# First attention of a two-block kernel: keys rotated on GpSimd, four tiles turned by VectorE blocks and GpSimd transfers, and one pair of late sums four units apart

## What is computed

```python
mod = (c @ w_mod[l] + b_mod[l]).reshape(B, N_MOD, D)
h = rms_norm(x, g_pre_mix[l]) * (1 + scale_m) + shift_m
proj = h @ w_in[l]
q_lat = rms_norm(proj[..., COL_QLAT:COL_K], q_lat_norm_g[l])
q = apply_rope((q_lat @ w_q_up[l]).reshape(B, S, ATTN_HEADS, HEAD_DIM), cos_a, sin_a)
k = apply_rope(proj[..., COL_K:COL_V].reshape(B, S, ATTN_HEADS, HEAD_DIM), cos_a, sin_a)
...
y_b = dsa_attention(q, k, v, q_idx, k_idx, idx_w)
gates = jax.nn.sigmoid(proj[..., COL_GATE:])
merged = gates[..., :D] * (y_a @ w_proj_a[l]) + gates[..., D:] * (y_b @ w_proj_b[l])
```

## Time and profile before

| | |
|---|---|
| median of 3 runs | 2350.73 us (2349.63 to 2352.76) |
| the profiled execution, own time | 2351.91 us |
| its span, first to last instruction | 2350.2 us |
| TensorE busy | 2333.5 us (99%) |
| VectorE busy | 1672.9 us (71%) |
| ScalarE busy | 1124.1 us (48%) |
| GpSimd busy | 415.2 us (18%) |
| mean granted TensorE clock | 0.999 of full speed |

### The profile page before, as it was taken

One profiled execution on the slowest core, in us unless ns is written; L12 is line 12 of the kernel. 1 busy time (PEld: TensorE's weight loads), 2 busy tenths in 40 slices (PEclk: granted clock), 3 DMA queues, 4 the chain that ended last, 5 costly groups with the idle time before them and its releaser, 6 DMA issues.

```text
span 2350.2 us, 31106 instructions
## 1 busy us (share of the span) xinstructions
PE 2333.5 (99%) x10647; PEld 1930.8 (82%) x10647; DVE 1672.9 (71%) x2138; ACT 1124.1 (48%) x1415; POOL 415.2 (18%) x824
## 2 busy tenths in 40 slices
PE   9999999999999999999999999999999999999998
PEld 7888788888888888888888888888888888888887
DVE  7998899999886666665544465676765577888764
ACT  4544546543554444444443445544744444544554
POOL 0001000024001211212100001111112135686310
PEclk9999999999999999999999999999999999999999
DMA  9985469999847877865655556666566666665564
GB/s 392 396 318 203 154 241 360 332 343 369 350 171 250 268 251 237 270 232 195 235 193 195 192 179 219 215 218 215 183 209 215 204 209 198 201 197 191 184 212 153
DMA packets 174106, 561.05 MB, mean 239 GB/s; under 512 B 29696, under 2 KB 34080, under 8 KB 173344
## 3 DMA queue, kind: packets, MB, share of 16 engines
q1 hardware_dynamic: 145584, 528.28, 65.1%
q0 software_dynamic: 25600, 22.33, 3.2%
q10 hardware_dynamic: 2800, 8.81, 1.1%
HBM read 534.91 MB, written 2.11 MB: 229 GB/s over the span
## 4 chain that ended last, share of the span: by engine, by line
PE 89%; DVE 6%; DMA 2%; issue 1%; ACT 1%; SPq 0%; ACTq 0%; DVEq 0%
PE acc L2409 27%; PE acc L2410 27%; PE acc L2416 27%; DVE lo L1397 2%; DVE macc L1433 2%; PE tb L2497 1%; DMA raw<-in_wa_dram 1%; DMA start_raw<-in_wa_dram 1%; PE tb L2940 1%; PE tb L2409 1%; PE tb L2410 1%; PE tb L2416 1%; PE acc L2467 0%; PE acc L2465 0%; PE acc L2466 0%
## 5 line engine op out<-in xcount | busy, mean ns | idle before, releaser
L1397 DVE TENSOR_TENSOR lo<-raw,hi 128x1024 fp32r<-128x1024 f32 x809 | 969.3, 1207 | 549.7 <-ACT hi L723 546.3
L723 ACT ACTIVATE hi<-raw 128x1024 fp32r<-128x1024 f32 x809 | 844.7, 1049 | 978.5 <-PE acc L2416 690.7
L2409 PE MATMUL acc<-hi,Hh 128*128 128x512 f32 x1960 | 773.7, 395 | 1.8 <-issue 0.9
L2410 PE MATMUL acc<-hi,Hl 128*128 128x512 f32 x1960 | 763.6, 390 | 0.0
L2416 PE MATMUL acc<-lo,Hh 128*128 128x512 f32 x1960 | 524.4, 389 | 0.0
L2409 PEld LDWEIGHTS acc<-hi,Hh 128*128 128x128 f32 x1960 | 368.1, 188 | 80.0 <-issue 4.8
L2416 PEld LDWEIGHTS acc<-lo,Hh 128*128 128x128 f32 x1960 | 367.9, 188 | 77.3
L2410 PEld LDWEIGHTS acc<-hi,Hl 128*128 128x128 f32 x1960 | 368.2, 188 | 75.9 <-issue 1.4
L2409 PE MATMUL acc<-hi,hbh 128*128 128x512 f32 x512 | 202.7, 396 | 0.0
L2410 PE MATMUL acc<-hi,hbl 128*128 128x512 f32 x512 | 199.6, 390 | 0.0
L638 POOL DMA_DIRECT2D tok<-sgt x176 | 86.2, 498 | 501.1 <-DVE sgt L1523 424.4
(11 more groups left out here) (374 smaller groups left out, 2270.7 us busy)
## 6 DMA issues: line engine op xcount, KB each, us to landing
raw<-in_wa_dram SPq DMA_DIRECT2D x680, 512.0 KB, 4.4
late_raw<-in_wa_dram SPq DMA_DIRECT2D x96, 512.0 KB, 6.0
raw<-in_wb_dram SPq DMA_DIRECT2D x96, 512.0 KB, 4.2
start_raw<-in_wa_dram SPq DMA_DIRECT2D x64, 512.0 KB, 7.7
raw<-in_wc_dram SPq DMA_DIRECT2D x64, 512.0 KB, 4.1
tok<-sgt POOLq DMA_DIRECT2D x384, 32.0 KB, 4.4
landed<-sgt POOLq DMA_DIRECT2D x192, 32.0 KB, 4.0
pt_landed<-att_parts POOLq DMA_DIRECT2D x192, 12.0 KB, 3.0
```

What stands on the lines that cost most here:

```text
L723: act.activation(hi[:, s, 0:n], raw[:, r, 0:n], ACT.Copy).then_inc(hi_ready, 1)
L1397: dve.tensor_tensor(lo[:, s, 0:n], raw[:, r, 0:n], hi[:, s, 0:n].bitcast(F32), ALU.subtract)\
L2409: pe.matmul(dst(tt), a, hi[:, s, w], start=first and i == 0, stop=False)
L2410: pe.matmul(dst(tt), b, hi[:, s, w], start=False, stop=False)
```

## The change

The two key parts are rotated in place by GpSimd (rotate_keys) as soon as they are summed; the first ahead of the index keys, the second behind them. For the two query tiles VectorE does the products and GpSimd the add (add_query). Each of the four tiles is then turned into blocks by VectorE (turn_first), moved by 16 transfers of GpSimd's queue and put in order into kT or qT by two copies on GpSimd (move_first). The buffers lie in sg. TensorE's four tiles of transposes and ScalarE's eight copies out of PSUM go. ScalarE waits for all four tiles before the first sigmoid, TensorE before the scores of head 0. Block 5's second half is transposed one unit later, after OUT0+26, and its two takes move to before OUT0+25 and OUT0+29.

```diff
-LATE_SUMS = [LATE[b * KD + KD - 1] + (6 if 2 <= b < 5 else 3) * half for b in range(LATE_WIDE) for half in range(2)]
-TAKES = [unit + 5 for unit in LATE_SUMS]
+LATE_SUMS = [LATE[b * KD + KD - 1] + (6 if 2 <= b < 5 else 4 if b == 5 else 3) * half for b in range(LATE_WIDE) for half in range(2)]
+TAKES = [unit + (3 if i // 2 == 5 else 5) for i, unit in enumerate(LATE_SUMS)]
...
+QIDX_TURNED = KX_COPIED + 3, KX_COPIED + 5
+KEYS_SUMMED = (QUARTERS - 1) * PARTS // 2 + 2
...
+        first_out = [sb(f"first_out{i}", [P, 4, TT * P], at=sg_at + (8 + 4 * i) * KB) for i in range(2)]
+        first_in = [sb(f"first_in{i}", [P, 4, TT * P], at=sg_at + (16 + 4 * i) * KB) for i in range(2)]
+        key_tmp = [sb(f"key_tmp{i}", [P, TT, N], at=sg_at + (16 + 4 * i) * KB) for i in range(2)]
...
+            def rotate_keys(n):
...
+                for tt in range(TT):
+                    pool.wait_ge(acc_free[tt], KEYS_SUMMED + n)
+                pool.tensor_tensor(tmp[:, :, :, 0:half], a[:, :, :, half:HD], spread(ropeS[:, :, 0:half]), ALU.mult)
+                pool.tensor_tensor(tmp[:, :, :, half:HD], a[:, :, :, 0:half], spread(ropeS[:, :, half:HD]), ALU.mult).then_inc(key_step, 1)
+                pool.wait_ge(key_step, 2 * n + 1)
+                pool.tensor_tensor(a, a, spread(ropeC[:]), ALU.mult).then_inc(key_step, 1)
+                pool.wait_ge(key_step, 2 * n + 2)
+                pool.tensor_tensor(a, a, tmp, ALU.add).then_inc(first_rotated, 1)
+
+            pool.wait_ge(const_in, 5 * 16)
+            rotate_keys(0)
             pool.wait_ge(rstd_ready, 3)
...
             pool.tensor_copy(kd[:, :, IDIM:], kd[:, :, 0:IDIM]).then_inc(kidx_ready, 1)
+            rotate_keys(1)
+
+            def move_first(n):
+
+                pool.wait_ge(first_blocks, n + 1)
+                if n > 1:
+                    pool.wait_ge(first_turned, n - 1)
+                for i in range(4):
+                    for j in range(4):
+                        pool.dma_start(first_in[n % 2][32 * j:32 * j + 32, i, :], first_out[n % 2][32 * i:32 * i + 32, j, :])\
+                            .then_inc(first_moved, 16)
+                pool.wait_ge(first_moved, MOVED * (n + 1))
+                dst, k = (kT, qT)[n // 2], n % 2 * 4
+                for tt in range(TT):
+                    at = slice(tt * P, (tt + 1) * P)
+                    ins = pool.tensor_copy(dst[:, k:k + 4, at].rearrange("p k (i t) -> p k i t", i=4),
+                                           first_in[n % 2][:, :, at].rearrange("p i (k t) -> p k i t", k=4))
+                ins.then_inc(first_turned, 1)
+
+            def add_query(t):
+
+                pool.wait_ge(query_parts, t + 1)
+                pool.tensor_tensor(tok[:, 1 - t], tok[:, 1 - t], sgt[:], ALU.add).then_inc(query_added, 1)
+
+            move_first(0)
+            add_query(0)
+            move_first(1)
+            add_query(1)
+            move_first(2)
+            move_first(3)
...
-            copy_tile(kT, 0)
-            split_to(QI3B + 2)
-            copy_tile(kT, 4)
...
-                if i == 6:
-                    copy_tile(qT, 0)
...
-                if i == 10:
-                    copy_tile(qT, 4)
...
                 if since == 0 and n >= 0:
+                    if n == 0:
+                        act.wait_ge(first_turned, 4)
                     finished(GATES0 + 8 * n + 7)
                     read_out(lambda tt: sg[:, tt, n * N:(n + 1) * N], n % 2, ACT.Sigmoid)
...
-            for tt in range(TT):
-                dve.wait_ge(acc_free[tt], (QUARTERS - 1) * PARTS // 2 + 2)
-            rotate(None, lambda tt: tok[:, 1, tt, :], 4, HD, HD // 2, ropeC, ropeS, src=lambda tt: part_at(0, tt))
...
-            for tt in range(TT):
-                dve.wait_ge(acc_free[tt], (QUARTERS - 1) * PARTS // 2 + 3)
-            rotate(None, lambda tt: tok[:, 0, tt, :], 4, HD, HD // 2, ropeC, ropeS, src=lambda tt: part_at(1, tt))
+
+            def turn_first(n):
+
+                if n < 2:
+                    dve.wait_ge(first_rotated, n + 1)
+                    src = lambda tt: part_at(n, tt)
+                else:
+                    dve.wait_ge(query_added, n - 1)
+                    dve.wait_ge(first_moved, MOVED * (n - 1))
+                    src = lambda tt: tok[:, 3 - n, tt, :]
+                for tt in range(TT):
+                    at = slice(tt * P, (tt + 1) * P)
+                    ins = dve.transpose(first_out[n % 2][:, :, at].rearrange("p j (k t) -> p j k t", k=4),
+                                        src(tt).rearrange("p (k j c) -> p j k c", k=4, j=4))
+                ins.then_inc(first_blocks, 1)
...
-                dve.wait_ge(tr_copy, TOK_TURNED[t])
-                dve.wait_ge(tok_ready, t + 2)
+                if t > 1:
+                    dve.wait_ge(tr_copy, QIDX_TURNED[t - 2])
+                if t == 3:
+                    dve.wait_ge(query_added, 1)
+                elif t > 0:
+                    dve.wait_ge(tok_ready, t)
...
-                    rotate(0, tile, 4, HD, HD // 2, ropeC, ropeS)
+                    rotate(0, tile, 4, HD, HD // 2, ropeC, ropeS, add=False)
+                    for tt in range(TT):
+                        dve.wait_ge(acc_free[tt], KEYS_SUMMED + 2 + t)
+                    dve.sem_inc(query_parts, 1)
...
             add_uv(4)
+            turn_first(0)
             turn_query(1)
+            turn_first(1)
...
+                if i == 9:
+                    turn_first(2)
...
             split_to(GATES0 + 10)
+            turn_first(3)
...
-            part_tile(q3, 0, after={1: lambda: turned(1)})
+            part_tile(q3, 0)
...
-            part_tile(q3, 1, after={0: lambda: turned(0)})
+            part_tile(q3, 1)
...
-            tile(qlath, qlatl, 0, 2, after={0: lambda: query_turned(1, 6), 1: lambda: logits(7)})
+            tile(qlath, qlatl, 0, 2, after={0: lambda: logits(6), 1: lambda: logits(7)})
...
+                if head == 0:
+                    pe.wait_ge(first_turned, 4)
...
-                if u == GATES0:
-                    turned(0)
```

More of the change, by code:

```diff
@@ L149 @@
 KX_COPIED = KD // 2 + 1
-TOK_TURNED = KX_COPIED + 2, KX_COPIED + 4, KX_COPIED + 7, KX_COPIED + 9
-COPIES_BEFORE_K2 = TOK_TURNED[3] + 4 + HEADS1
+QIDX_TURNED = KX_COPIED + 3, KX_COPIED + 5
+COPIES_BEFORE_K2 = QIDX_TURNED[1] + HEADS1
+KEYS_SUMMED = (QUARTERS - 1) * PARTS // 2 + 2
 QB = A_UNITS
@@ L410, in two_blocks @@
         merged_tok = sem("merged_tok")
+        key_step = sem("key_step")
+        first_rotated = sem("first_rotated")
+        query_parts = sem("query_parts")
+        query_added = sem("query_added")
+        first_blocks = sem("first_blocks")
+        first_moved = sem("first_moved")
+        first_turned = sem("first_turned")
         hid_blocks = sem("hid_blocks")
@@ L595, in _ @@
                                pattern=[[0, 8], [1, P]], channel_multiplier=-1).then_inc(ws_ready, 1)
+            def rotate_keys(n):
+                heads = lambda ap: ap.rearrange("p t (h d) -> p t h d", h=4)
+                spread = lambda ap: ap.unsqueeze(2).to_broadcast([P, TT, 4, ap.shape[-1]])
+                half = HD // 2
+                a, tmp = heads(k_part[:, n]), heads(key_tmp[n][:])
+                for tt in range(TT):
[8 more added lines that the diff above has]
+            rotate_keys(0)
             pool.wait_ge(rstd_ready, 3)
@@ L607, in _ @@
             ih = IROPE // 2
-            pool.wait_ge(const_in, 5 * 16)
             pool.wait_ge(kn_step, 3)
@@ L1494, in layer_norm_stats, with rotate @@
                 inverse_root()
-            def rotate(pair, dst, heads, dim, half, cos, sin, width=N, src=None, done=tok_ready):
+            def rotate(pair, dst, heads, dim, half, cos, sin, width=N, src=None, done=tok_ready, add=True):
                 h4 = lambda ap: ap.rearrange("p (h d) -> p h d", h=heads)
@@ L1512, in rotate @@
                         ins.then_inc(acc_free[2 * pair + tt], 1)
+                if not add:
+                    return
                 for tt in range(TT):
```

## The result

| | kernel before | changed kernel |
|---|---|---|
| median of 5 runs | 2350.73 us (2349.58 to 2352.76) | 2360.86 us (2359.75 to 2363.78) |
| ratio, 95% interval | | 1.0042 (1.0031 to 1.0054) |
| the profiled execution, own time | 2351.91 us | 2363.78 us |
| its span | 2350.2 us | 2362.1 us |
| mean granted TensorE clock | 0.999 | 0.997 |

The account below looks back on a forecast made before the run. TensorE was taken to bound the kernel. Transposes -3.5, standstill +7.6, clock +1.7 and late sums -1.0 gave +4.8 us, with VectorE and GpSimd's queue at nothing: 2355.5 us against the median of 2350.73, range 2350.0 to 2359.5.

Parts of the forecast that it names:

- The bound: Whole kernel: TensorE, busy 2333.5 of 2350.2 us, sets the time; any new gap is paid in full.
- Transposes, -3.5 us: Four tiles of transposes removed from TensorE, 0.87 us each, all on the path: 3.48 us won.
- VectorE, nothing: VectorE's changed work costs nothing: net relief in a stretch where TensorE never waited for it.
- Rival 3: VectorE and GpSimd hold each other up, as at 207 to 280 us: 4 us lost, 2359.5 us; chance 0.13.
- GpSimd's queue, hidden: GpSimd's queue before the last tile costs 0: tile 3 finds it free with 4 us to spare.
- The standstill, +7.6 us: TensorE stands still before unit GATES0+11 while ScalarE waits for the last tile: 7.6 us, bounds 2.6 to 9.4.
- The clock, +1.7 us: TensorE's clock falls to 1.2 GHz behind the standstill, costing 1.7 us, bounds 0 and 2.7.
- The late sums, -1.0 us: Block 5's moved sums remove TensorE's 1.46 us wait at 642.78; 0.45 is lost again: 1.0 won, bounds 0.3 and 1.46.
- Sum: All terms together: +4.8 us, 2355.5 us against the median, range 2350.0 to 2359.5.

Follow-up runs that it names:

- cut: Changed kernel with GpSimd's key rotations and query additions cut into pieces of 128 elements a partition (24 and 8 instructions); 2354.43 us, ratio 1.0008.
- rot_dve: Changed kernel with both key rotations and both query additions back on VectorE, GpSimd keeping transfers and copies; 2357.82 us, ratio 1.0025.
- turns_spread: rot_dve with VectorE's block transposes of query tile 2 behind logits step 7 and tile 3 behind step 11; 2351.83 us, ratio 1.0002.
- pool_reads: Kernel before plus four scratch additions of two 128x1024 SBUF tiles on GpSimd behind its index keys; 2357.30 us, ratio 1.0025.
- warm_gap: Changed kernel with 60 unused transposes on TensorE behind unit GATES0+10, where it stood still; 2360.68 us, ratio 1.0040.
- tile3_early: Changed kernel with VectorE's block transposes of tile 3 moved from behind the GATES0+9 split to behind the twelfth logits step; 2355.36 us, ratio 1.0017.
- turns_early: rot_dve with VectorE's block transposes of query tile 2 behind logits step 5 and tile 3 behind step 9; 2351.90 us, ratio 1.0001.
- cut_spread: cut with VectorE's block transposes of tile 2 behind logits step 7 and tile 3 behind step 11; 2349.88 us, ratio 0.9991.
- after_again: The changed kernel itself run and traced once more; 2361.16 us, ratio 1.0039.
- sums_undone: Changed kernel with the late sums of block 5 put back where they were before; 2361.61 us, ratio 1.0042.
- spread_old_sums: turns_spread with the late sums of block 5 where they were before; 2351.80 us, ratio 0.9999.
- cut_vector_adds: cut_spread with the two query additions back on VectorE; 2349.02 us, ratio 0.9985.

## Why the prediction was wrong

**The bound** held: TensorE 99% busy, every new gap paid in full, and whatever it lost ahead of 485 us stayed lost (the ledger's +10.3 at 316 us is still +10.3 at 534).

**Transposes, -3.5 us: the size was right, not the place where it can be had.** With nothing in the way (cut) TensorE is 4.3 us ahead at 311 us: 3.5 for the transposes, the 0.43 of issue time behind the first that I had left out, and 0.4 more. But it was had only where VectorE was relieved as well. With the rotations on VectorE (rot_dve, turns_spread) the gain of the two key tiles is gone by 236 us (the ledger stands at 0.0 there in turns_spread): the row of turns_spread above is TensorE waiting 1.33 us for VectorE until 216.8, which is the 0.87 us of the removed tile and the 0.43 behind it, to the very time at which it went on before (216.74, behind the earlier trace rows). The row that was to tell me this is `216.31 0.43 issue`: a gap behind the transposes means that they were not what TensorE's next step waited for. VectorE's timeline of before has what it waited for, an addition that ends at 216.64:

```profile
215.36 1.28 DVE L1683 TENSOR_TENSOR v<-acc,v 128x512 f32<-128x512 f32 x2
```

So "a stretch where TensorE never waited for it" was wrong too.

**VectorE, nothing: wrong, the largest miss, and the step that failed.** Rival 3 was the truth, and bigger than I had priced it: 4 us there, and 5.8 and 5.6 here (cut's -4.3 against +1.5 and +1.3). I had the row that speaks for it and the ten GpSimd instructions that would do the same, and gave it 0.13 since VectorE was to be relieved of 4 us a rotation. The relief is there and isn't enough: the pair of splits that starts at 234.59 and ends at 236.94 in the trace of before starts at 232.86 and ends at 239.60 in that of the changed kernel, so 4.4 us of waiting in one pair eat up the time won and more. My own estimate of 3.6 us for a long instruction would have given the size: a pair that meets two of them can wait up to 7.2 us beyond its own 2.35. I also wrote that no GpSimd instruction of that trace is longer than 1.8 us; line 630 has some of up to 2.69 (at 523.2). The Trainium skill (SBUF — State Buffer, Who interferes with whom) states this exclusion for whole instructions, against GpSimd's reads and not its writes; 6.74 us for a pair in place of 2.35, the 2.68 us addition that ends with GpSimd's, nothing lost beside fills and 0.5 instead of 5.7 us with short pieces agree with it.

**GpSimd's queue, hidden: right for the changed kernel**, with 6.7 us to spare before tile 3 (its idle time at 308.33) where I had 4. The copies took 1.2 to 1.5 us for my 2.0. A GpSimd instruction of 1024 elements took 2.4 to 2.5 us where it started first and 3.3 where a two-input instruction of VectorE was already running, for my 3.6.

**The standstill, +7.6 us: 6.4, by two errors that cancel.** From the end of the blocks (308.05) to the rounded unit (320.69) it took 12.6 us for my 17.1: the transfers 9.1 for 12.8, the copies 1.2 for 2.0. My row pair was taken where more traffic ran (250 and 332 GB/s in its first two stretches of 4 us, against 182 and 197 here); in the other runs the same sixteen transfers took 9.1 to 11.8 us. Against that, TensorE finished its unit 6.3 us behind the blocks, not 9.6. I had let VectorE shift with TensorE, as both wait for the logits; in fact VectorE was late by itself. rot_dve, without GpSimd's arithmetic, has it nearly as late (blocks at 304.15, TensorE out of work at 310.75, 6.6 us), so most of it is not GpSimd's doing. Take VectorE's lead as the time from the end of its split of a unit to TensorE's last group of that unit. For GATES0+9 it is 7.0 us before, 3.7 in the changed kernel and 4.0 in rot_dve, but 6.8 in pool_reads, where TensorE is 5.6 us late and nothing is turned or moved: a late TensorE does take VectorE with it, but the new work on VectorE takes lead away besides. In rot_dve 2.9 us of lead are missing ahead of tile 2's block transposes (at 282 us) and 3.0 behind them, so those are not the cause. 1.2 us are missing right behind the block transposes of tile 1 (at 253 us), 1.8 at 264 and 3.3 at 268; 0.9 of the last step is TensorE's own gain from the third tile, and what makes the rest is open.

**The clock, +1.7 us: 2.4 and 2.2**, from the ledger's rise less the wait; 1.9 to 2.1 by warm_gap's trace. Inside the bounds.

**The late sums, -1.0 us: none that the medians show.** Their wait was of one execution, 0.6 us on average, and in part of the executions the last halves took back more than that. (The cover there was smaller too: the split at 651.36 takes 1.22 us, so 0.23 and not 0.31.)

**Sum.** Of the miss of 5.3 us in the median, 5.0 is the stretch up to 311 us, +1.0 the sums, and -0.5 the standstill with the clock (8.8 for 9.3); the rest is within what single executions differ. The range ended at a rival 3 of 4 us with everything else as forecast. Its real size and no gain from the sums would have put the end near 2362, but that is known only now.

## What to carry to other kernels

Moving elementwise work with two SBUF inputs to GpSimd was not free for VectorE; look which of VectorE's instructions will stand beside it, who waits for those, and cut GpSimd's work into short instructions before anything else. A transpose taken off the bounding engine is won only if the other engines are ahead there too: a gap right behind the removed piece says that they aren't. Work put into another engine's queue pushes back all that stands behind it there, and each link of that may be waited for: check the whole queue, not only the piece that moves. A term that rests on one wait in one execution needs the same wait in a second trace, or a range that begins at nothing.

## What the runs showed of the hardware

- A pair of VectorE splits (128x1024, two SBUF inputs) took 2.35 us alone, 4.55 beside GpSimd additions of 128x1024, 6.74 in the changed kernel, 2.6 to 2.9 beside additions of 128x128, and 2.35 beside fills. The 128x128 additions took 0.67 us each in that company (21.30 for 32) and the large ones 2.96 (11.83 for 4), so cutting cost GpSimd 1.8 times the time.
- TensorE's granted clock fell behind waits of 1.80 (tile3_early), 1.94 (turns_early), 2.20 (cut_spread), 5.4 (cut), 6.0 (rot_dve) and 6.4 us, each time behind a busy stretch; behind the 1.46 us wait of the earlier trace rows, the 1.33 us wait of turns_spread and the 1.93 us wait of pool_reads it stayed at 1.00. So the length of the wait alone doesn't decide, and what does is not shown here. A fall cost 1.7 to 2.4 us (the ledger's rise less the wait), whether the wait before it was 1.8 or 6.4 us long.
- Sixteen SBUF to SBUF transfers issued by GpSimd took 9.1 to 11.8 us from the first issue to the copy that read them; issuing them alone took 7.8 to 8.1. For the last tile it was 9.1 wherever they ended in the long wait or in its place (changed, after_again, sums_undone, warm_gap, rot_dve, cut), 10.1 in turns_early, and 11.1 to 11.8 in tile3_early, cut_spread, turns_spread, spread_old_sums and cut_vector_adds. In the changed kernel, rot_dve and cut the core's DMA moved 182 to 201 GB/s in the two stretches of 4 us behind the first issue; each of turns_early, tile3_early, cut_spread, turns_spread and cut_vector_adds has a stretch of 284 to 325 GB/s there. More traffic beside them would explain the difference; no run changes the traffic alone.
